# Scores one unit sooner in TensorE's program of a hybrid attention and convolution trunk

## What is computed

```python
z = rms_norm(x, g) @ w_in
ya = neighbourhood_attention(q, k, v, rpb) * silu(ag)   # 4 heads, windows of 8 x 16 in an 8 x 64 grid
yb = dilated_attention(rotary(q), rotary(k), v) * silu(bg)   # 6 heads, three patterns of windows
yc = conformer_conv(a, b, ...) * silu(cg)   # 31 taps per channel, LayerNorm, pointwise product
x = x + concatenate([ya, yb, yc]) @ w_out
```

## Time and profile before

| what | value |
|---|---|
| median of 3 runs | 514.31 us (513.91 to 514.74) |
| the profiled execution | 513.27 us |
| its span, first to last instruction | 511.4 us |
| TensorE busy | 502.9 us, 98% |
| VectorE busy | 365.4 us, 71% |
| ScalarE busy | 275.5 us, 54% |
| POOL busy | 164.6 us, 32% |
| granted TensorE clock, mean | 0.998 |

### The profile page before, as it was taken

One profiled execution on the slowest core, in us unless ns is written; L12 is line 12 of the kernel. 1 busy time (PEld: TensorE's weight loads), 2 busy tenths in 40 slices (PEclk: granted clock), 3 DMA queues, 4 the chain that ended last, 5 costly groups with the idle time before them and its releaser, 6 DMA issues.

```text
span 511.4 us, 10087 instructions
## 1 busy us (share of the span) xinstructions
PE 502.9 (98%) x3902; PEld 405.4 (79%) x3902; DVE 365.4 (71%) x741; ACT 275.5 (54%) x531; POOL 164.6 (32%) x224
## 2 busy tenths in 40 slices
PE   8999999999999999999999999999999999999995
PEld 7888787887877778788888888878787777778883
DVE  6899978899984666521739878887999656852424
ACT  6834667664664475522525447676646646752314
POOL 0023332221143557424511333222122356663101
PEclk9999999999999999999999999999999999999999
DMA  8815889669986997999602378985999979999974
GB/s 280 317 46 125 205 210 193 145 161 227 221 210 156 222 253 170 251 238 270 164 2 82 87 164 192 206 189 99 210 231 216 232 165 270 208 235 238 211 183 164
DMA packets 55119, 97.78 MB, mean 191 GB/s; under 512 B 19872, under 2 KB 33696, under 8 KB 55072
## 3 DMA queue, kind: packets, MB, share of 16 engines
q0 software_dynamic: 19648, 62.93, 54.3%
q1 hardware_dynamic: 35136, 34.02, 23.8%
q10 hardware_dynamic: 288, 0.19, 0.1%
HBM read 84.92 MB, written 5.90 MB: 178 GB/s over the span
## 4 chain that ended last, share of the span: by engine, by line
PE 96%; DMA 1%; issue 1%; POOL 0%; ACT 0%; DVE 0%; POOLq 0%; ACTq 0%
PE acc L607 23%; PE acc L608 22%; PE acc L609 22%; PE sc L716 5%; PE tp L749 4%; PE misc L780 2%; PE sc L669 2%; PE sc L607 1%; PE sc L609 1%; PE sc L608 1%; PE sc L671 1%; PE sc L670 1%; DMA w_lo<-w_out 1%; PE misc L775 1%; PE misc L791 1%; PE misc L806 1%
## 5 line engine op out<-in xcount | busy, mean ns | idle before, releaser
L607 PE MATMUL acc<-act_hi,w_hi 128*128 128x512 f32 x480 | 194.4, 405 | 0.0
L608 PE MATMUL acc<-act_hi,w_lo 128*128 128x512 f32 x480 | 187.7, 391 | 0.0
L609 PE MATMUL acc<-act_lo,w_hi 128*128 128x512 f32 x480 | 187.2, 390 | 0.0
L607 PEld LDWEIGHTS acc<-act_hi,w_hi 128*128 128x128 f32 x480 | 90.2, 188 | 21.9 <-issue 3.9
L609 PEld LDWEIGHTS acc<-act_lo,w_hi 128*128 128x128 f32 x480 | 90.2, 188 | 20.0
L608 PEld LDWEIGHTS acc<-act_hi,w_lo 128*128 128x128 f32 x480 | 90.3, 188 | 16.9 <-issue 0.5
L875 ACT ACTIVATE w_lo<-w_hi 128x1024 fp32r<-128x1024 f32 (+1 forms) x62 | 61.9, 999 | 47.7 <-DMA w_hi<-w_out 38.2
L1090 POOL DMA_DIRECT2D w_lo<-w_in x40 | 35.9, 897 | 106.6 <-ACT w_lo L875 106.0
L1318 DVE SCALAR_TENSOR_TENSOR y<-ub,par,y 128x512 f32<-128x512 f32 x90 | 69.8, 776 | 0.0
L1318 DVE SCALAR_TENSOR_TENSOR ub<-ub,par 128x512 f32<-128x512 f32 x84 | 63.2, 752 | 0.0
L937 ACT ACTIVATE prob<-prob,nmx 128x384 f32<-128x384 f32 (+1 forms) x80 | 45.3, 566 | 25.7 <-DVE nmx L1340 25.5
(11 more groups left out here) (150 smaller groups left out, 725.4 us busy)
## 6 DMA issues: line engine op xcount, KB each, us to landing
w_hi<-w_in POOLq DMA_DIRECT2D x40, 512.0 KB, 5.7
w_lo<-w_in POOLq DMA_DIRECT2D x40, 512.0 KB, 6.4
w_hi<-w_out POOLq DMA_DIRECT2D x16, 512.0 KB, 6.3
w_lo<-w_out POOLq DMA_DIRECT2D x16, 512.0 KB, 6.9
pT<-w_in SPq DMA_DIRECT2D x15, 512.0 KB, 4.5
v<-v_way SPq DMA_DIRECT2D x40, 112.0 KB, 5.6
v_way<-vs SPq DMA_DIRECT2D x24, 112.0 KB, 5.2
gf<-nabias SPq DMA_DIRECT2D x20, 128.0 KB, 5.9
```

The costliest lines, as they stand in the source:

```text
L607: nc.tensor.matmul(to[:, :], w_hi[:, slot, k, :], a_hi[:, k, :], start=i == 0, stop=False)
L608: nc.tensor.matmul(to[:, :], w_lo[:, slot, k, :], a_hi[:, k, :], start=False, stop=False)
L609: last = nc.tensor.matmul(to[:, :], w_hi[:, slot, k, :], a_lo[:, k, :], start=False, stop=i == K - 1)
```

## The change

The batch of scores for unit n is issued in TensorE's program of unit n - 2, where it was in that of unit n - 1. Within a unit its place stays the same: behind the half projection tile, in front of values and turn. So batches for units 4, 8, 12, ... 36 move from units 3, 7, 11, ... 35 to units 2, 6, 10, ... 34. In units 10, 18 and 26, which hold the values of pairs 0, 1 and 2, scores now stand directly in front of them. The first batch (unit 0, ahead of the loop) doesn't move. The programs of the other engines are unchanged.

```diff
                     if n < UNITS:
                         in_tile(l, tile_at(n)[0], n % 2 * KD // 2, (n % 2 + 1) * KD // 2)
 
-                        if n + 1 < UNITS and (n + 1) % 4 == 0:
-                            scores(l, n + 1)
+                        if n + 2 < UNITS and (n + 2) % 4 == 0:
+                            scores(l, n + 2)
                     else:
```

## The result

| what | before | after |
|---|---|---|
| median (lowest to highest), runs | 514.11 us (513.12 to 514.74), 6 | 517.73 us (516.89 to 521.63), 6 |
| the profiled execution, its span | 513.27, 511.4 | 517.62, 515.8 |

The ratio is 1.0082, 95% interval 1.0062 to 1.0102, or 3.2 to 5.2 us. The forecast was +2.2. Its direction was right, and so was its main cause; the size was about half of what came (3.6 between the medians, 4.2 by the ratio).

The account below looks back on a forecast made before the run. TensorE, busy 502.9 of 511.4 us, was taken to bound the kernel. Per layer a 1.55 us wait less 3 x 0.15 for switches gives 1.10; two layers add 2.2 to 514.31, forecasting 516.5 us, range 514.8 to 518.2.

Parts of the forecast that it names:

- The wait at unit 20: Unit 20's scores, now in unit 18, wait for VectorE's maximum of unit 19 and start 1.55 us late per layer.
- its cost part: Section on moved scores waiting for VectorE's maxima: only unit 20 late, by 1.43 us before overheads; VectorE can't catch up.
- copies and exponentiates behind the same turn, with idle to spare: ScalarE's work behind the delayed turn of unit 16, in unit 18, was taken to have idle enough.
- There are two ways to change it: TensorE's time changes only by instructions taking less or more, or by a wait that isn't there today.
- The switch: In units 10, 18 and 26, scores in front of values save one array shape switch, 0.15 us each; bounds 0 to 0.30.
- Behind the wait: After unit 20's wait, VectorE is held up about 1.0 us for pair 1's values; unit 24 keeps 0.8 of room.
- rival B: The wait repeats at scores of units 24 and 28, some 0.8 us more per layer: +3.8, 518.1 us; chance 0.10.
- rival A: VectorE keeps up, no wait arises and only switches count: 513.4 us, or 512.5 with 0.30 each; 0.05 faster, 0.06 within 0.2%.
- C: The wait is smaller or partly absorbed in the 0.3 us weight tile wait, switches give 0.30: +0.7, 515.0 us; chance 0.06.
- Unit 16: Its moved scores find the maximum done with 0.16 us of room; a small wait there would not add.
- the sign that was named for unit 20: In the profile after, TensorE's weight load for unit 20's scores idles about 1.9 us, 0.36 of it the switch.
- No DMA is issued in them: The nine moved score groups issue no DMA, so SP's and POOL's queues keep their order.

Follow-up runs that it names:

- unit 20 alone: Against the kernel before, only the scores of unit 20 issued one unit sooner, the other eight groups as before: 517.48 us, 1.0062.
- the filled kernel before: The kernel before with 128 already met waits added to TensorE's program among products of tiles 2 to 8 of layer 0: 514.12 us, 0.9997.
- values first: Against the kernel before, only scores of units 12, 20 and 28 moved, to units 10, 18 and 26, behind the pair's values: 517.49 us, 1.0063.
- all but 20, filled: All score groups but unit 20's one unit sooner than in the kernel before, plus 128 already met waits in TensorE's program: 518.35 us, 1.0066.
- all but 20: Against the kernel before, all score groups one unit sooner except unit 20's: 517.46 us, 1.0059.

## Why the prediction was right in direction and half the size

- **The wait at unit 20: right.** One per layer, on the maximum of unit 19, 1.55 us without the other moves, measured as 1.55 in the kernel with unit 20 alone.
- **What failed** is the sentence in its cost part "The turn of unit 9 itself comes 0.15 sooner (one switch less), and with it all of VectorE to unit 20". Its first half came true (the maximum of unit 13, which waits for that turn, came 0.12 sooner), its second didn't: VectorE came 0.44 later instead, so that unit 20's scores were 1.99 late and not 1.40. Its own next wait, for POOL's product at L1282, was missed: I followed VectorE and TensorE from the moved group, and ScalarE ("copies and exponentiates behind the same turn, with idle to spare") only behind unit 18. The turn of unit 8 in unit 10 is moved just as much, and behind it hangs a chain over ScalarE and POOL with 1.15 us of room. That cost 0.59 us per layer, 1.2 in all, of which 0.7 is shown by undoing it.
- **The sum had no term for the supply of instructions** (0.8) nor for the weight tile near the end (0.5). The second may be scatter: waits for tiles of `w_out` add up to 0.2 to 2.1 us in the twelve profiles, and to 0.9 in the filled kernel before, which has no change in it. "There are two ways to change it", work or a wait on another engine, left out this third one. The changed kernel's other runs, up to 521.63, leave room for more than the profiled one shows: the execution of 521.63 has a mean granted clock of 0.994 where the first four have 0.997 or 0.998. No trace of it was kept.
- **The switch: right.** Between 64x32 and 128x32 the load idles 0.20 (0.41 in unit 26), and a merge gives 0.12 to 0.14 (0.15 forecast). The rule of the Trainium skill (TensorEngine Tiling (Array Packing), Key Properties) that a change of mode drains TensorE agrees with that idle. It is too small to matter.
- **Behind the wait: right.** VectorE waited for pair 1's values (1.89 in layer 0, where the break adds 0.8, and 1.08 in layer 1; the forecast had 1.0), and units 24 and 28 got no wait, so rival B fell; rival A fell at once. C fell too: the weight tile absorbed nothing.
- **Unit 16** waited 0.6 (0.94 with the switch), where the forecast had 0.16 of room and named any such wait over 0.2 a sign against it. It comes of the same 0.44. As the forecast said of a wait there, it doesn't add: its cost is inside the 1.99. But it hides the failure in the sign that was named for unit 20, an idle of about 1.9: the load idles 1.85 as forecast, because TensorE arrives as late as VectorE does. Only the position, 71.07 against 69.08, shows it.
- **"No DMA is issued in them"** is true of the groups, but the landing of v in front of pair 1's values was checked nowhere, and in layer 1 it has 0.56 us of room. The changed kernel got by with the scores in front; values first did not.
- Unit 13's maximum was forecast at 103.7 and came at 103.45, which is 103.76 on the clock of the kernel before; the longer idle for the turn didn't come (0.49, before 0.67), since VectorE reached unit 12 later than thought.

## What to carry to other kernels

When a group is put ahead of others in an engine's queue, go through what it delays one by one, and follow each to the end of its chain over the other engines, also at places where the wait in question is not. Merging groups of small instructions saves a switch of 0.12 us, but makes a stretch in which a block of 256 instructions is used up in less time than the next takes to come (3.4 us against 4.2 here); count where the edges fall, and whether a stretch of small instructions holds two of them, and look for pauses inside a run of like instructions that wait for nothing. The result of a variant can hang on the luck of such an edge: before judging by it, shift the stream, and count where the shift puts the edges in every such stretch.

## What the runs showed of the hardware that I had not expected

TensorE can be out of instructions in an unrolled program without branches: 0.6 to 2.8 us, at block edges alone, ending 2.2 to 2.5 us after the block's transfer begins. The Trainium skill, Runtime: NRT & Kernel Launch, section Instruction fetch mechanics, calls the cost of a 16 KiB edge mostly hidden; the profiled runs bear that out at all but one of their 31 edges at most, but that one cost 0.6 to 2.8 us, in a change that is worth 3.6.

A wait of some 2 us can cost more than its length. In "values first" TensorE idled 2.1 us in front of layer 1's values, and from 379.9 on its granted clock was at the lower of its two levels (1.2 GHz) for 3.4 us. The stretch 381.0 to 382.6 of it, and the chain of waits there:

```profile
381.00:382.60 1.60, 1.60 (x39) 1.60 (x35) 1.47 (x4) 0.00 (x0) 0.88 (x1) 0.50 0.94 357
```

```profile
377.12 2.13 issue
379.26 1.38 PE misc L775 x32
380.64 3.11 PE misc L780 x64
```

The values took 4.49 us where they take 1.01 + 1.75 = 2.76 at full clock, so 1.7 us came on top of 2.1. The same 3.4 us at half clock followed the break of 2.3 in "all but 20, filled"; it did not follow the 2.8 of "all but 20", nor the changed kernel's waits of 1.4.
